# Twelve pairs of gate tiles of the first block as seven half-size products

## The reference, cut to what is touched

```python
h = rmsnorm(x, norm_mix_pre[l])
proj = h @ w_in[l]                      # 1024 -> 7168
(q, k, v, g_ret, sc_b, sc_c, sc_x, cf_a, cf_b, gate_logits) = split(proj)
y_ret = (silu(g_ret) * head_groupnorm(retention(rotary(q), rotary(k), v))) @ w_ret_out[l]
y_sc = (sc_b * causal_dwconv(sc_c * sc_x)) @ w_sc_out[l]
c = silu(layernorm(causal_dwconv(cf_a * sigmoid(cf_b), 31 taps)))
y_cf = c @ w_cf_out[l]
gates = sigmoid(gate_logits).reshape(B, S, 3, 1024)
merged = gates[:, :, 0] * y_ret + gates[:, :, 1] * y_sc + gates[:, :, 2] * y_cf
x = x + rmsnorm(merged @ w_o[l], norm_mix_post[l])
```

## Time and profile before

| | us |
|---|---|
| median of 3 runs | 3080.21 (3079.84 to 3081.51) |
| the profiled execution | 3080.47, span 3079.2 |
| TensorE busy | 3070.0 (100%) |
| VectorE busy | 2029.2 (66%) |
| ScalarE busy | 1400.2 (45%) |
| GpSimd busy | 619.4 (20%) |

### The profile page before, as it was taken

One profiled execution on the slowest core, in us unless ns is written; L12 is line 12 of the kernel. 1 busy time (PEld: TensorE's weight loads), 2 busy tenths in 40 slices (PEclk: granted clock), 3 DMA queues, 4 the chain that ended last, 5 costly groups with the idle time before them and its releaser, 6 DMA issues.

```text
span 3079.2 us, 40010 instructions
## 1 busy us (share of the span) xinstructions
PE 3070.0 (100%) x15812; PEld 2624.5 (85%) x15812; DVE 2029.2 (66%) x2728; ACT 1400.2 (45%) x2197; POOL 619.4 (20%) x514
## 2 busy tenths in 40 slices
PE   9999999999999999999999999999999999999999
PEld 8888888888888888888888889988888888998887
DVE  6876456667787655666768766657656765755864
ACT  4333334335433333443555544536645554444752
POOL 1202212341121121234213301120011420211001
PEclk9999999999999999999999999999999999999999
DMA  4684546556667454555664464657552254564443
GB/s 172 217 238 163 141 165 189 170 154 216 202 205 226 174 148 151 192 178 164 187 204 172 123 202 141 183 161 182 160 185 98 81 157 155 174 176 126 134 131 133
DMA packets 153962, 517.92 MB, mean 168 GB/s; under 512 B 17680, under 2 KB 17936, under 8 KB 143312
## 3 DMA queue, kind: packets, MB, share of 16 engines
q1 hardware_dynamic: 139040, 419.18, 40.2%
q0 software_dynamic: 13440, 91.46, 14.0%
q10 hardware_dynamic: 1296, 4.72, 0.5%
HBM read 488.55 MB, written 140.51 MB: 204 GB/s over the span
## 4 chain that ended last, share of the span: by engine, by line
PE 97%; DVE 2%; ACT 1%; DMA 0%; SPq 0%; issue 0%; POOL 0%; DVEq 0%; POOLq 0%
PE ps L682 95%; PE ps L776 1%; PE ps L1138 1%; DVE r L1934 0%; DVE f L1939 0%; DVE wl L1924 0%; DMA raw<-wsum 0%; DVE f L2002 0%; SPq L2964 0%; DMA X<-x_in 0%; ACT wh L1258 0%; PE ps L726 0%; DVE f L2070 0%; ACT L1295 0%; DVE f L2276 0%
## 5 line engine op out<-in xcount | busy, mean ns | idle before, releaser
L682 PE MATMUL ps<-h,wh 128*128 128x512 f32 (+1 forms) x5568 | 1521.5, 360 | 0.4 <-DVE wl L1924 0.2
L682 PEld LDWEIGHTS ps<-h,wh 128*128 128x128 f32 x5568 | 993.4, 188 | 162.3 <-issue 2.6
L682 PE MATMUL ps<-h,wl 128*128 128x512 f32 (+1 forms) x2784 | 1000.4, 359 | 0.0
L1924 DVE TENSOR_TENSOR wl<-raw,wh 128x1024 fp32r<-128x1024 f32 (+2 forms) x655 | 787.2, 1211 | 263.1 <-ACT wh L1258 259.3
L1258 ACT CAST wh<-raw 128x1024 fp32r<-128x1024 f32 (+2 forms) x668 | 645.1, 981 | 425.9 <-PE ps L682 402.1
L682 PEld LDWEIGHTS ps<-h,wl 128*128 128x128 f32 x2784 | 522.7, 188 | 78.7
L682 PE MATMUL ps<-r,wh 128*128 128x512 f32 x1536 | 474.5, 390 | 1.0 <-DVE r L1934 0.6
L682 PEld LDWEIGHTS ps<-r,wh 128*128 128x128 f32 x1536 | 284.9, 188 | 59.1 <-issue 2.2
L682 PE MATMUL ps<-r,wl 128*128 128x512 f32 x792 | 304.3, 389 | 0.0
L1355 ACT CAST r<-f 128x512 fp32r<-128x512 f32 (+1 forms) x194 | 114.5, 596 | 401.4 <-DVE f L2374 169.0
L2841 POOL TENSOR_TENSOR f<-f,f 128x512 f32<-128x512 f32 x64 | 107.2, 1675 | 670.3 <-DVE f L2188 670.3
(11 more groups left out here) (218 smaller groups left out, 3161.5 us busy)
## 6 DMA issues: line engine op xcount, KB each, us to landing
raw<-wst SPq DMA_DIRECT2D x376, 512.0 KB, 4.2
raw<-wsum SPq DMA_DIRECT2D x120, 512.0 KB, 4.2
raw<-wpr SPq DMA_DIRECT2D x74, 512.0 KB, 3.9
wsum<-wpr POOLq DMA_DIRECT2D x31, 1024.0 KB, 8.9
wsum<-wsum POOLq DMA_DIRECT2D x62, 512.0 KB, 5.9
raw<-wst SPq DMA_DIRECT2D x48, 320.0 KB, 3.2
raw<-wpr SPq DMA_DIRECT2D x38, 256.0 KB, 3.0
r<-r SPq DMA_DIRECT2D x64, 128.0 KB, 2.3
```

Source lines behind the costliest of these rows:

```text
L682: return e.matmul(o, a, b, start=start, stop=stop, skip_group_check=True)
L1924: e.tensor_tensor(l[:, 0:WIDTH[c]], source(c), h[:, 0:WIDTH[c]].bitcast(F32), ALU.subtract).then_inc(*lo_cut.up(("lo", c)))
```

## The change

It makes six pairs of gate tiles in each of the first block's two layers by `two_tiles`: tiles 4 to 7 of branch 1 and 0 to 7 of branch 2 (SINGLE says how many tiles of a branch stay single: 8, 4, 0). The 12 pairs get blocks and sums, 74 blocks in all in place of 62.
- GpSimd's `mix` runs in mixer1 too, ahead of the rotations; `all_roped`, given to it as `more`, stands between the combinations "4" and "3". In layer 0 it needs no saved rows (x_in has them); in layer 1 `save_rows(2)` goes first.
- ScalarE and VectorE split "1" and "6" at ca2 and ca3, "4" at k0 and "3" in the g loop behind `query_key(1)` (`mixed_hi`, `mixed_lo`), ahead of g's sigmoid and product.
- `rows_back` runs for every boundary behind gate2_6; `renew` waits for it.
- `sum_slot`s: mixer1 14 in place of 8 (the four at layer 1's start go), the FFN two of three j in place of one of two, two more at an FFN boundary, and every j in place of every second one in the second block's za loop. 12 block copies more are issued by SyncE: at q, k and v of layer 0 and at the pairs' chunks; those at gate1_4 and gate1_6 go.
- `ln_out` stands for tile 0 at gate0_7 as before, for tile 1 behind the pair 4, 5 of branch 1 and for 2 and 3 behind the pair 6, 7. The tile of ones goes to buffer 61, computed at `ln_split` after the last retention.
- Gate tiles of branches 1 and 2 have the buffers in GATE_AT.

```diff
@@ -46,6 +46,7 @@
+SINGLE = {0: 8, 1: 4, 2: 0}
@@ -93,11 +94,14 @@
         for b, w in enumerate(("w_ret_out", "w_sc_out", "w_cf_out")):
-            one(f"gate{b}_", D1["gate"] + 1024 * b, 0)
+            if SINGLE[b]:
+                one(f"gate{b}_", D1["gate"] + 1024 * b, 0)
             for j in range(8):
-                if j < 7:
+                if j < SINGLE[b] - 1:
...
                 if j % 2 == 0:
+                    if j >= SINGLE[b]:
+                        two_tiles(f"{l}/gate{b}_{j}", A, l, *(D1["gate"] + 1024 * b + (j + i) * P for i in range(2)))
@@ -360,7 +365,7 @@
         put(t, f"{L}/gate0_7", [[("ln_sum", L)], [("ln_split", L)], [("ln_centre", L)], [], [("ln_split2", L)], [("ln_root", L)], []]
-            + [[("ln_out", L, j)] for j in range(4)])
+            + [[("ln_out", L, 0)]])
@@ -392,6 +397,9 @@
+GATE_AT = {1: (66, 67, 68, 66, 60, 61, 67, 68), 2: (62, 63, 64, 65, 60, 61, 66, 67)}
@@ -401,6 +409,7 @@
 GATE_RING = {"b": (68, 47, 48, 46, 67), "a": (64, 65, 66, 67), "c": (64, 65, 26, 27, 66, 67)}
+LN_OUT = {(1, 4): (1,), (1, 6): (2, 3)}
@@ -556,11 +565,14 @@
             if L < 2:
-                return F(66 + j % 3)
+                return F(GATE_AT[b][j] if b else 66 + j % 3)
...
+            if L < 2 and j >= SINGLE[b]:
+                return {1: (("done", ("o", L, 3)), ("gated", L, 1, 2)), 2: (("cf_lo", L, 3),) * 2 + (("gated", L, 1, 5), ("gated", L, 1, 6))}[
+                    b][(j - SINGLE[b]) // 2]
@@ -617,9 +629,11 @@
         def ones_at(L):
-            name = f"ones{max(L, 1)}"
+            if L < 2:
+                return R(61)[:, 0:P]
+            name = f"ones{L}"
             if name not in views:
-                offset = base + 4 * (NB * S + 7 * CH) if L < 2 else vt_at + 4 * ((L % 2 + 1) * NV - P)
+                offset = vt_at + 4 * ((L % 2 + 1) * NV - P)
@@ -887,22 +901,30 @@
                 n = AHEAD[b]
-                for j in range(n):
+                for j in range(min(n, SINGLE[b])):
                     tile(f"{L}/gate{g}_{j}", xs)
-                for j in range(8):
-                    if j + n < 8:
-                        tile(f"{L}/gate{g}_{j + n}", xs)
+                def some(j, ks):
                     key = ("pr", L, b, j)
...
                     h, l = weights(name)
-                    o = take(key)
-                    for k in range(4):
+                    o = bank(key) if ks[0] else take(key)
+                    for k in ks:
                         w.wait_ge(*at(*ready, k))
-                    last = group(o, h, l, [(j % 2 * 4 + k) * P for k in range(4)], ys)
-                    closes = (("closed", NAME[name]),) if j % 2 else ()
-                    last.then_inc(*group_done.up(("done", key), *closes))
+                    last = group(o, h, l, [(j % 2 * 4 + k) * P for k in ks], [ys[k] for k in ks], ks[0] == 0, ks[-1] == 3)
+                    if ks[-1] == 3:
+                        closes = (("closed", NAME[name]),) if j % 2 else ()
+                        last.then_inc(*group_done.up(("done", key), *closes))
+                for j in range(SINGLE[b]):
+                    if j + n < SINGLE[b]:
+                        tile(f"{L}/gate{g}_{j + n}", xs)
+                    some(j, range(4))
+                for j in range(SINGLE[b], 8, 2):
+                    slot(f"{L}/gate{g}_{j}*0")
+                    two_tiles(L, f"{L}/gate{g}_{j}", lambda i: some(j + (i > 0), (range(4), range(2), range(2, 4))[i]))
@@ -1287,6 +1309,9 @@
                     acc, hi, _ = SUM_AT["ln"]
+                    if not second:
+                        w.wait_ge(*at("done", ("o", L, 3)))
+                        ones(L)
@@ -1451,17 +1476,26 @@
             def gate_proj(L, b, cut_merged=None):
-                for j in range(AHEAD[b]):
+                for j in range(min(AHEAD[b], SINGLE[b])):
                     slot(f"{L}/gate{b}_{j}")
-                for j in range(8):
-                    if j + AHEAD[b] < 8:
+                for j in range(SINGLE[b]):
+                    if j + AHEAD[b] < SINGLE[b]:
                         slot(f"{L}/gate{b}_{j + AHEAD[b]}")
...
                     gate_sigmoid(L, b, j)
+                for j in range(SINGLE[b], 8, 2):
+                    c = NAME[f"{L}/gate{b}_{j}*0"]
+                    cut(c + 3)
+                    two_gates(L, b, j, lambda: cut(c + 4), lambda: cut(c + 5), lambda i: cut(c + 6 + i))
+                    if (b, j) in LN_OUT:
+                        for i in LN_OUT[b, j]:
+                            small_step("ln_out", L, i)
                     if cut_merged and j:
+                        cut_merged(j - 2)
                         cut_merged(j - 1)
                 if cut_merged:
+                    cut_merged(6)
                     cut_merged(7)
@@ -1546,9 +1580,13 @@
                         *act_tile.up(("glu_gate", L, j), ("free", key)))
+                    if j > 1:
+                        mixed_hi(L, "16"[j - 2])
...
                     copied(f"{L}/{nm}{j}", F(ROPE_T[0][r]), ("to_rotate", L, r))
+                    if r == 1:
+                        mixed_hi(L, "4")
@@ -1569,6 +1607,7 @@
                         query_key(1)
+                        mixed_hi(L, "3")
@@ -1624,6 +1663,10 @@
+            def mixed_hi(L, m):
+                w.wait_ge(*at("mixed", L, m))
+                e.copy(mixed(m, 0), mixed("3", int(m == "3"), F32)).then_inc(*act_hi.up(("mixed_hi", L, m)))
@@ -2189,18 +2228,34 @@
             def gate_proj(L, b, cut_merged=None):
-                for j in range(AHEAD[b]):
+                for j in range(min(AHEAD[b], SINGLE[b])):
                     slot(f"{L}/gate{b}_{j}")
-                for j in range(8):
-                    if j + AHEAD[b] < 8:
+                for j in range(SINGLE[b]):
+                    if j + AHEAD[b] < SINGLE[b]:
                         slot(f"{L}/gate{b}_{j + AHEAD[b]}")
...
                     gated(L, b, j)
+                for j in range(SINGLE[b], 8, 2):
+                    c = NAME[f"{L}/gate{b}_{j}*0"]
+                    cut(c + 3)
+                    four_parts(f"{L}/gate{b}_{j}", gate_at(L, b, j), gate_at(L, b, j + 1), lambda: cut(c + 4), lambda: cut(c + 5))
+                    cut(c + 6)
+                    gated(L, b, j)
+                    cut(c + 7)
+                    gated(L, b, j + 1)
+                    if (b, j) in LN_OUT:
+                        for i in LN_OUT[b, j]:
+                            small_step("ln_out", L, i)
                     if cut_merged and j:
+                        cut_merged(j - 2)
                         cut_merged(j - 1)
                 if cut_merged:
+                    cut_merged(6)
                     cut_merged(7)
+            def mixed_lo(L, m):
+                lo_part(mixed("3", int(m == "3"), F32), mixed(m, 0), mixed(m, 1), at("mixed_hi", L, m), ("mixed_lo", L, m))
@@ -2283,8 +2338,12 @@
                         *dve_tile.up(("glu", L, j), ("free", key)))
-                for nm, j in (("q", 0), ("k", 0), ("q", 1), ("k", 1)):
+                    if j > 1:
+                        mixed_lo(L, "16"[j - 2])
+                for r, (nm, j) in enumerate((("q", 0), ("k", 0), ("q", 1), ("k", 1))):
                     slot(f"{L}/{nm}{j}")
+                    if r == 1:
+                        mixed_lo(L, "4")
@@ -2751,9 +2810,11 @@
             def boundary(B):
-                if B > 4:
+                if B not in FFN:
...
                 gains(B)
+                for _ in range(2 if B in FFN else 0):
+                    sum_slot()
@@ -2797,10 +2858,10 @@
-                w.wait_ge(*at("done", (PAIRS[-1] if B == 6 else PAIRS[len(PAIRS) // 2 - 1], "c21")))
-                e.dma_start(X[:, 0:8 * S], kept_x).then_inc(*landed(f"back{B}"))
-            def mix(L, B):
+                w.wait_ge(*at("done", (f"{LAYER[B]}/gate{'c' if B > 4 else 2}_6", "c21")))
+                e.dma_start(X[:, 0:8 * S], x_in if B == 1 else kept_x).then_inc(*landed(f"back{B}"))
+            def mix(L, B, more=lambda: None):
@@ -2814,8 +2875,10 @@
-                w.wait_ge(*at("p", L, 1, 3))
-                w.wait_ge(*at("landed", f"kept{B}"))
+                if L > 1:
+                    w.wait_ge(*at("p", L, 1, 3))
+                if B:
+                    w.wait_ge(*at("landed", f"kept{B}"))
@@ -2827,6 +2890,7 @@
                 step(A, A, h_quarter(1, 0, 1), ALU.add, ("mixed", L, "4"), seen("4", 0))
+                more()
@@ -2851,13 +2915,16 @@
                 e.dma_start(vt[:, 1 - L, 0:n], vec[L + 1][:, 0:n]).then_inc(*landed(f"vec{L + 1}"))
-                for _ in range(4 if L else 0):
-                    sum_slot()
-                for r in range(4):
-                    roped(L, r, 52)
+                def all_roped():
+                    for r in range(4):
+                        roped(L, r, 52)
+                if L:
+                    save_rows(2)
+                mix(L, 2 * L, all_roped)
                 for h in range(4):
```

(17 more changed lines are left out.)

8 lines of the change are left out of this document (3 added, 5 removed).

## The result

| | before | changed |
|---|---|---|
| median | 3080.74 (4 runs, 3079.84 to 3081.51) | 3126.15 (4 runs, 3125.34 to 3128.0) |
| profiled execution, span | 3080.47, 3079.2 | 3126.14, 3124.8 |
| ratio to before, 95% interval | | 1.0148 (1.0131 to 1.0166) |

The changed kernel is 45.4 us slower. 3108.5 was forecast, with a range to 3121: the sign was right, the size was not, and the time lies 5 us above the range.

The account below looks back on a forecast made before the run. TensorE, busy for 3070.0 of 3079.2 us, was taken to bound the kernel. Forecast: 3080.5 - 10.9 (columns) + 11.3 + 15 (layer starts) + 12.6 (norm's tiles) = 3108.5 us, own range 3094 to 3116, full range 3082 to 3121.

Parts of the forecast that it names:

- Gain, 10.9: Columns taken out of TensorE by making gate tiles in pairs: 0.91 us a pair, 6 pairs in each of 2 layers.
- The starts, 11.3 and 15: GpSimd's combinations slow VectorE in mixer1; TensorE waits for spread and first decay product: 11.3 us layer 0, 15 layer 1.
- the first combination, priced at 4: Layer 1's start: six GpSimd instructions beside a nearly full VectorE add 4 us on the same chain.
- upper bound: If the weights' lateness in layer 1 adds fully, some 6 us more: 3114.
- The norm's tiles, 12.6: Waits for ScalarE's copies: 4.9 us before branch 2's gates, 1.4 at gate1_6; 6.3 a layer, 12.6 in all.
- What I cost at nothing: Rows read back, added sums, block copies, ScalarE's casts and loads, all taken as covered by slack: 0 us.
- 1 us and 6 more on TensorE: Slack claimed for the six extra sums in mixer1 ahead of the layer norm's sum, so they cost nothing.
- The third rival: TensorE's clock falls to its lower level around the waits, losing 9 to 18 us; with 12, 3120; chance 0.14.
- Hidden after all: Rival: TensorE waits nowhere, so the kernel is faster at 3069.6; chance 0.10 for 3069.6 to 3074.
- only the norm's tiles: Rival: only the norm's tiles wait, combinations cost 0.2 us a layer; 3083, no change; chance 0.13.
- The sums come late: Rival: GpSimd's queue delays the layer norm's sum by 5 us or so, 0 to 3 reaching TensorE; 3111; chance 0.06.
- what would show it: Signs: waits of some 40 us at layer starts and near branch 2's gates; taps beside GpSimd taking 1.7 us.

Follow-up runs that it names:

- a3: The changed kernel with combinations 6, 4 and 3 made behind the rotations and head statistics, between the sums, and split at sb0, sb1 and sb3: 3114.31 us.
- a4: The changed kernel with norm tile 1 behind gate tile 2 of branch 1, tiles 2 and 3 inside pairs 4, 5 and 6, 7: 3105.86 us.
- a1: The changed kernel with the two sums at each end of an FFN moved into the FFN's loop (j = 3 and 9): 3119.18 us.
- b1: The changed kernel with the edits of a1, a3, a4 and c1 together: 3081.94 us (10 runs), ratio 1.0006.
- b2: b1 with two sums fewer (layer 0) and four fewer (layer 1) ahead of the norm's sum, combination 3 split behind gate tile 0 of branch 0: 3071.2 us.
- a5: The changed kernel with added products, results overwritten, keeping TensorE at work through four waits in each layer: 3120.24 us (3115.43 to 3126.02).
- a2: The changed kernel with only combination 3 made after the last head's statistics and split at sb1, behind the g loop: 3115.07 us.
- b4: b2 with combination 3 made two sums later and split behind gate tile 2 of branch 0: 3068.34 us, ratio 0.9963.
- c1: The changed kernel with one more ScalarE activation of 128 columns, where the kernel before computed its tile of ones: 3122.51 us.

## Why the prediction was wrong

| term | forecast | measured, by the lag |
|---|---|---|
| columns | -10.9 | -10.4 |
| the two starts | 26.3 | 28.9 |
| the norm's tiles | 12.6 | 20.8 |
| two sums at the end of each FFN | 0 | 8.2 |
| the rest of the program | 0 | -1.9 |
| sum | 28.0 | 45.6 |

The row of the norm's tiles is the steps 4.8 and 5.6 with the columns' 10.4 added.

**Gain, 10.9:** 10.4 measured, 0.87 a pair in place of 0.91. Right within 5%.

**The starts, 11.3 and 15:** 13.9 and 15.0 measured, with the mechanisms named (GpSimd's instruction costing VectorE 1.03, the spread first and the decay product behind it, each within 2 us of its forecast time). The forecast was of the lateness at the first decay product. There the lag is 12.1 in layer 0, and layer 1 adds 12.4; the other 1.8 and 2.6 are slow columns behind it. In layer 0 the table load was missing, 1.3 us, since I did not think of it when the tile of ones moved, and 0.6 of the lag is there before the first instruction that changed. In layer 1 the 15.0 is luck: the first combination, priced at 4, cost 0.0 where it stood alone (a3), and the clock filled its place. With the other combinations there was a wait of 1.76 for weights at 886, which the forecast had only in its upper bound, and some 5 us of the step are clock.

**The norm's tiles, 12.6:** the waits were 14.7, right within 2.1; with the clock behind them 20.3 went (a4).

**"What I cost at nothing".** This step failed, the first of two. The prediction counted 18 sums more and gave a cover only for the six in mixer1; the two at each end of an FFN stood in the diff and got no line, no cover and no price. The four of them cost 8.2 us by the lag, 7.0 by a1, for loads that landed in 7.5 us where they had 4.6. Of the six, the cover of "1 us and 6 more on TensorE" was a fair reading: as soon as TensorE was on time, they cost waits of 3.9 and 10.2 us in b1's profiled execution and 10.7 by the medians of b1 and b2 (b2 also splits combination 3 later, which no run separates). In the changed kernel that loss was hidden under the others.

**The clock.** This is the second step that failed: the sum priced every wait at its own length and the clock at nothing. The third rival was what happened, with 19.4 us of slow columns where 9 to 18 was its band and 12 its price. All waits together were even a little shorter than forecast, 36.6 against 38.9, though 8.1 of them were for weights, at four places that were not in the sum. I had made the rival 0.14 likely, against a sum that had six waits of 5 us or so in it; that the clock was 1.00 in the kernel before, where TensorE hardly rests, was no reason against it. With 12 for the clock and 8 for the sums the forecast would have been 3128.5, against 3126.1.

**The other rivals.** "Hidden after all" and "only the norm's tiles" were wrong. "The sums come late" was there but covered. Of the list of what would show it most held: the waits that it named stood where it said, and a tap beside GpSimd took 5.06 / 3 = 1.69 us for the 1.7. It did not name the four waits for weights, at 41, 746, 886 and 1545 us.

## What to carry to other kernels

Count every instruction that an edit adds, at its own place in its queue: the combinations were costed to the tenth, and two DMAs of 0.9 us to issue, at the end of each of two FFNs, cost 4 us each time because they ran beside loads without slack. A late TensorE covers the next lateness, so losses appear one behind the other: mend, look again, and judge the idea only when no wait is left; here the same matmuls take 3126 or 3068 us by where 14 GpSimd instructions, 3 norm tiles and some sums of each layer stand, and by one small activation. And price a forecast wait with its clock: here 36.6 us of waits came with 19.4 of slow columns; filling four of the waits in each layer gave 5.9 us back by the medians, 7.4 in the profiled execution.

## What the runs showed that I had not expected

- ScalarE's table load ran either at 25.7 to 26.1, ahead of the wait of the activation it serves, or at 36.7, behind it, by whether another activation stood ahead of that wait. Removing an unrelated 0.33 us activation put the load's 1.28 us on TensorE's path.
- The clock fell behind each rest of 2.37 us and more in the changed kernel, as at 746 (2.37 us, 0.67 from 745 to 750). In other runs a rest of 2.78 us left it at 1.00 (a5, ending at 128) and one of 1.87 lowered it (a1, a2, a3).
- GpSimd's "1" in layer 1, beside a VectorE busy for 12.69 of 14 us, cost TensorE nothing: the lag did not move from 1.90 in b1. That the weights' time in hand paid for it is likely, but no run shows it.
- What stays open: why a5's runs spread over 11 us and b1's over 11.5, where the kernel before and b4 stay within 5. The clock goes with it: the mean granted clock of b1's three longest executions (3086.8 to 3089.3) is 0.997, of its two shortest (3077.8 and 3078.6) 0.999; of a5's it is 0.997 at 3126.0 and 0.999 at 3115.4. So the clock falls in more of the time in one execution than in another of the same kernel, and a difference of a few us between two kernels with rests, as c1's, can be that. No run separates it.
